# Third attention of a two-block transformer: scores from high and low parts of queries and keys, queries turned one block row ahead

## The reference, cut to what matters

```python
q = (rms_norm_2(c_q, mla_q_norm[j]) @ mla_w_uq[j]).reshape(b, s, N_TOK_HEADS, QK_DIM)
q = jnp.concatenate([q[..., :QK_NOPE], apply_rope(q[..., QK_NOPE:], positions)], axis=-1)
kv = (rms_norm_2(c_kv, mla_kv_norm[j]) @ mla_w_ukv[j]).reshape(
    b, s, N_TOK_HEADS, QK_NOPE + V_DIM)
k_nope, v = kv[..., :QK_NOPE], kv[..., QK_NOPE:]
k_rope = apply_rope(k_r[:, :, None, :], positions)
k = jnp.concatenate(
    [k_nope, jnp.broadcast_to(k_rope, (b, s, N_TOK_HEADS, QK_ROPE))], axis=-1)
tok = causal_attention(q, k, v).reshape(b, s, TOK_WIDTH)
```

```python
sc = jnp.einsum('bqhd,bkhd->bhqk', q_blk, k, preferred_element_type=jnp.float32) * scale
sc = jnp.where(mask[None, None], sc, -jnp.inf)
p = jax.nn.softmax(sc, axis=-1).astype(v.dtype)
return jnp.einsum('bhqk,bkhd->bqhd', p, v)
```

## Time and profile before

| what | value |
|---|---|
| median of 3 runs | 3132.32 us (3131.62 to 3132.63) |
| the profiled execution | 3131.1 us, its span 3129.0 us |
| PE busy | 3066.4 us, 98% of the span |
| DVE busy | 1791.4 us, 57% |
| ACT busy | 1329.6 us, 42% |
| the third attention, first score to last | about 2418.8 to 2705 us of the span |

### The profile page before, as it was taken

How to read it: one execution, slowest core, us unless ns; L and a number is a source line. 1 busy time by engine, 2 the same in 40 slices (tenths; PEclk the granted TensorE clock), 3 DMA queues, 4 the chain that set the end, 5 groups by cost and what they waited for, 6 DMA issues and landing times.

```text
span 3129.0 us, 50323 instructions
## 1 busy us (share of the span) xinstructions
PE 3066.4 (98%) x18600; PEld 2608.8 (83%) x18600; DVE 1791.4 (57%) x3573; ACT 1329.6 (42%) x2637; POOL 664.3 (21%) x886
## 2 busy tenths in 40 slices
PE   7999999999999999999999999998999999999999
PEld 7988888999999888888788888888977777787777
DVE  6657674353344322345888887876353666753675
ACT  5446565454445221232333333454433555522552
POOL 3423334453542000001111111001101011032240
PEclk9999999999999999999999999999999999999999
DMA  5110011011111321122233225643100000221012
GB/s 204 37 48 18 21 35 51 28 62 44 56 59 46 103 78 51 45 95 97 72 109 109 102 101 204 196 151 140 46 28 22 16 28 15 108 72 67 28 61 101
DMA packets 77412, 231.27 MB, mean 74 GB/s; under 512 B 17712, under 2 KB 21936, under 8 KB 65648
## 3 DMA queue, kind: packets, MB, share of 16 engines
q1 hardware_dynamic: 77168, 228.05, 20.8%
HBM read 183.92 MB, written 43.84 MB: 73 GB/s over the span
## 4 chain that ended last, share of the span: by engine, by line
PE 90%; DVE 6%; ACT 2%; issue 1%; DMA 1%; SPq 0%; POOL 0%; DVEq 0%; ACTq 0%; POOLq 0%
PE ps L2546 71%; PE ps L2589 7%; PE ps L2597 3%; PE ps L2553 2%; PE ps L2604 2%; PE ps L2620 2%; PE ps L2612 1%; PE ps L2623 1%; PE ps L2640 1%; DVE wlo L2815 0%; DVE hlo L2892 0%; ACT hhi L2660 0%; ACT whi L2650 0%; DVE qk L2923 0%; DMA fa2r<-scratch_fs 0%
## 5 line engine op out<-in xcount | busy, mean ns | idle before, releaser
L2546 PE MATMUL ps<-whi,hhi 128*128 128x256 f32 (+2 forms) x1920 | 580.5, 302 | 3.0 <-DVE hlo L2892 1.7
L2546 PE MATMUL ps<-whi,hlo 128*128 128x256 f32 (+2 forms) x1920 | 563.7, 294 | 0.0
L2546 PE MATMUL ps<-wlo,hhi 128*128 128x256 f32 (+2 forms) x1920 | 563.4, 293 | 0.0
L2546 PEld LDWEIGHTS ps<-whi,hhi 128*128 128x128 f32 x1920 | 368.2, 192 | 12.8 <-issue 5.1
L2546 PEld LDWEIGHTS ps<-wlo,hhi 128*128 128x128 f32 x1920 | 368.8, 192 | 7.4 <-issue 0.2
L2546 PEld LDWEIGHTS ps<-whi,hlo 128*128 128x128 f32 x1920 | 368.2, 192 | 7.7
L2546 PE MATMUL ps<-hhi,whi 128*128 128x512 f32 x864 | 342.3, 396 | 0.0
L2546 PE MATMUL ps<-hhi,wlo 128*128 128x512 f32 x864 | 337.0, 390 | 0.0
L2546 PE MATMUL ps<-hlo,whi 128*128 128x512 f32 x864 | 336.3, 389 | 0.0
L3154 POOL TENSOR_SCALAR stats<-stats 128x2 f32<-128x2 f32 (+2 forms) x230 | 59.3, 258 | 1194.1 <-ACT xsf L2654 509.1
L3143 POOL CAST whi<-raw 128x512 fp32r<-128x512 f32 (+4 forms) x180 | 113.7, 631 | 865.8 <-PE ps L2546 856.1
(11 more groups left out here) (616 smaller groups left out, 6996.6 us busy)
## 6 DMA issues: line engine op xcount, KB each, us to landing
raw<-in_W SPq DMA_DIRECT2D x61, 1024.0 KB, 4.8
scratch_fs<-fo SPq DMA_DIRECT2D x77, 256.0 KB, 2.0
raw<-in_W SPq DMA_DIRECT2D x24, 768.0 KB, 4.3
wd<-in_WD SPq DMA_DIRECT2D x44, 256.0 KB, 3.5
wf0b<-in_WF SPq DMA_DIRECT2D x10, 1024.0 KB, 5.3
wf1b<-in_WF SPq DMA_DIRECT2D x10, 1024.0 KB, 5.2
scratch_x<-x SPq DMA_DIRECT2D x16, 512.0 KB, 3.3
orw<-scratch_outs SPq DMA_DIRECT2D x6, 1024.0 KB, 5.8
```

Of the source, the lines that this page charges most:

```text
L2546: x = e.matmul(r.out, a, b, start=(r.start and m == 0), stop=(r.stop and m == n - 1), skip_group_check=r.joined)
```

## The change

1. Keys are kept as high and low part: `mkT[z, s, 0]` and `mkT[z, s, 1]`. ACT copies the high part out of PSUM, then DVE subtracts it from PSUM into the low part ("mk_out", and "kr_turn" for the rotated rows that all heads share). Two of the low parts lie in the unused ends of the second weight buffer, so the weights that follow the last projection into that buffer wait for the end of pair 4's scores.
2. Queries are no longer turned in the projection. `mq` is double buffered, and at the start of the scores of each double step `q_turn` turns the two blocks (both heads) of the next double step: PE 2 turns, ACT the high part (96 x 256), DVE the low part (96 x 256).
3. Scores are three passes: high x high, high x low, low x high. For five blocks the pieces are 2+3 instead of 4+1.
4. The turned probabilities are copied by DVE one time in three (`dve_turns=3`), not one in two.
5. The portions of the projections are spread anew over the steps: for odd p every second step, for even p in ten steps in a row.

```diff
@@ Att.probs @@
-                    r.by_dve = self.dve_turns and self.turn % 2 == 1
+                    r.by_dve = self.dve_turns and self.turn % self.dve_turns == 1
@@ q_turn, new @@
+        def q_turn(n):
+            p, qt = n // 8, 7 - n % 8
+            q = Rec()
+            q.place, q.rotated, q.free = DB.take(), q_rotated[p], flat(h_free, kr_places[1].full, q_used.get(n - 2))
+            q.src = [mq[p % 2][:, qt, s * 96:s * 96 + 96] for s in range(2)]
+            q.hi, q.lo = [x[0:96, :] for x in mqT[n % 2]]
+            q.hi_done = signal("mq_hi")
+            emit("mq_turn", q)
+            q_read[n] = q.place.read
@@ proj @@
-                evac(b, [(mkT[z_][s][0:64, cut], b.ps[64 * s:64 * s + 64, :]) for s in range(2)], set_q(p))
+                k = Rec()
+                k.place, k.free, k.hi_done = b, set_q(p), signal("mk_hi")
+                k.hi, k.lo = [[mkT[z_, s, x][0:64, cut] for s in range(2)] for x in range(2)]
+                emit("mk_out", k)
                 yield
-            for s in range(2):
-                for t0 in (0, 4):
-                    q = Rec()
-                    q.place, q.rotated, q.free = DB.take(), r.done, set_q(p)
-                    q.src = [mq[:, t0 + j, s * 96:s * 96 + 96] for j in range(4)]
-                    q.dst = mqT[z_][s][0:96, t0 * 128:t0 * 128 + 512]
-                    emit("mq_turn", q)
-                    yield
@@ units of the third attention @@
-                    for k0 in range(0, qt + 1, 4):
+                    first = 2 if qt == 4 else 4
+                    for k0, n in ((0, min(first, qt + 1)), (first, qt + 1 - first)):
...
+                    if s == 0 and at_q < 47:
+                        u.begin = lambda: q_next(at_q)
@@ fills_m @@
-                for n in range(1 if p % 2 == 0 else 3):
-                    yield
-                yield from proj(p)
-                for n in range(1 if p % 2 == 0 else 3):
+                yield
+                yield
+                for n, _ in enumerate(proj(p)):
+                    yield
+                    if p % 2 and n < 6:
+                        yield
+                for n in range(4 if p % 2 == 0 else 2):
                     yield
@@ steps loop @@
+            if i == 80:
+                spl_free[1] = [p_last[0], pairs[4][-1].s_full]
+                w_split()
@@ tensor, "scores" @@
-                        for p in r.parts:
-                            x = e.matmul(p.place.ps[:, o:o + n], *p.blocks[b], start=True, stop=True)
+                        passes = ((0, 0), (0, 1), (1, 0)) if isinstance(r.parts[0].blocks[b][0], tuple) else (None,)
+                        for j in passes:
+                            for p in r.parts:
+                                q, k = p.blocks[b] if j is None else (p.blocks[b][0][j[0]], p.blocks[b][1][j[1]])
+                                x = e.matmul(p.place.ps[:, o:o + n], q, k, start=j == passes[0], stop=j == passes[-1])
@@ vector, new kinds @@
+                elif kind == "mq_turn":
+                    w.wait_ge(*w.last)
+                    w.wait_ge(*r.hi_done)
+                    e.tensor_tensor(r.lo, r.place.ps[0:96, 0:256], r.hi.bitcast(F), ALU.subtract).then_inc(w.sig(r.place.read), 1)
+                elif kind == "mk_out":
+                    w.wait_ge(*r.hi_done)
+                    for s, (hi, lo) in enumerate(zip(r.hi, r.lo)):
+                        w.wait_ge(*w.last)
+                        a = e.tensor_tensor(lo, r.place.ps[64 * s:64 * s + 64, :], hi.bitcast(F), ALU.subtract)
+                        a.then_inc(w.sig(r.place.read) if s else w.inner(), 1)
```

More of the change, by code:

```diff
@@ L645, in build, with __init__ @@
         class Att:
-            def __init__(self, E, PT, os_, sb, ob, dve_turns=True, together=False, paired=False, by_feature=False, between=False):
+            def __init__(self, E, PT, os_, sb, ob, dve_turns=2, together=False, paired=False, by_feature=False, between=False):
                 self.by_feature, self.between = by_feature, between
@@ L683, in scored @@
                         r.blocks = list(zip(q, rhs)) if isinstance(q, list) else [(q, rhs)]
-                        r.n = sum(k.shape[-1] for _, k in r.blocks)
+                        r.n = sum(width(k) for _, k in r.blocks)
                         r.out, r.mx = u.E[:, at_[x]:at_[x] + r.n], mxs[x][:, p:p + 1]
@@ L2198, in proj @@
                 if hf:
-                    r.done = signal("q_rotated")
+                    r.done = q_rotated[p] = signal("q_rotated")
                     emit("q_rotated", r)
@@ L2224, in proj @@
                 yield
-            ch.done(m)
+            if p == 5:
+                p_last.append(m)
+            else:
+                ch.done(m)
         proj0, kr_places = proj(0), []
@@ L2236, in first_proj @@
             kr_places.append(load("tabM", tabM[:, :], d["tabM"], place.full))
-            kr_places.append([load(f"kr{s}", mkT[1][s][64:96, :], mkT[0][s][64:96, :], place.read, h_free) for s in range(2)])
+            kr_places.append([load(f"kr{s}{x}", mkT[1, s, x][64:96, :].bitcast(F), mkT[0, s, x][64:96, :].bitcast(F), kr_places[0].read, place.read, h_free)
+                              for s in range(2) for x in range(2)])
             yield from proj0
@@ L2242, in build @@
         drain(fill)
-        kr_tok, t_tabM = [kr_places[1].read, kr_places[3]], kr_places[2]
+        kr_tok, t_tabM = [[x.read for x in kr_places[:2]], kr_places[3]], kr_places[2]
         n_done[:] = [mem_us[-1].v_full, mem_us[-1].fin, mem_us[-1].s_full]
-        attM = Att([x[:, :] for x in mE], [x[:, :] for x in mPT], [x[:, :] for x in mO], SB2, OB2, paired=True)
+        attM = Att([x[:, :] for x in mE], [x[:, :] for x in mPT], [x[:, :] for x in mO], SB2, OB2, paired=True, dve_turns=3)
         for s_ in (attM.E, attM.PT, attM.O):
@@ L2586, in _ @@
                     for b in range(len(r.parts[0].blocks)):
[L2587 to L2591 removed]
+                        n = width(r.parts[0].blocks[b][1])
+                        passes = ((0, 0), (0, 1), (1, 0)) if isinstance(r.parts[0].blocks[b][0], tuple) else (None,)
[3 more added lines that the diff above has]
+                                x = e.matmul(p.place.ps[:, o:o + n], q, k, start=j == passes[0], stop=j == passes[-1])
+                                if b == len(p.blocks) - 1 and j == passes[-1]:
+                                    x.then_inc(p.place.full[0], 1)
                         o += n
@@ L2770, in _ @@
                     w.wait_each(r.free)
-                    for x, dst in enumerate(r.dsts):
+                    for x, dst in enumerate(r.dsts[0]):
                         w.wait_ge(*w.last)
                         a = e.activation(dst, r.place.ps[64:96, :], ACT.Copy)
-                        a.then_inc(w.sig(r.place.read) if x == 1 else w.inner(), 1)
+                        a.then_inc(w.sig(r.hi_done) if x == 1 else w.inner(), 1)
                 elif kind == "mq_turn":
@@ L2778, in _ @@
                     w.wait_each(r.free)
-                    e.activation(r.dst, r.place.ps[0:96, :], ACT.Copy).then_inc(w.sig(r.place.read), 1)
+                    e.activation(r.hi, r.place.ps[0:96, 0:256], ACT.Copy).then_inc(w.sig(r.hi_done), 1)
+                elif kind == "mk_out":
+                    w.wait_ge(*r.place.full)
+                    w.wait_each(r.free)
+                    for s, dst in enumerate(r.hi):
+                        w.wait_ge(*w.last)
+                        a = e.activation(dst, r.place.ps[64 * s:64 * s + 64, :], ACT.Copy)
+                        a.then_inc(w.sig(r.hi_done) if s else w.inner(), 1)
                 elif kind == "ln_stats":
```

69 lines of the change are left out of this document (44 added, 25 removed).

## The result

The changed kernel takes 3172.34 us, median of 4 runs (3172.11 to 3175.02), against 3131.97 us for the kernel before beside it (4 runs, 3126.87 to 3132.63). The ratio is 1.0133, with a 95% interval from 1.012 to 1.0146: 40.4 us slower, where 18 were forecast, and beyond the range's end at 3162. The profiled execution has a span of 3170.3 us.

What follows compares the result with a forecast made beforehand. PE bounds the kernel now (98% busy); after, a DVE-ACT loop and key stalls add 2.9 + 2.1 + 2.4 + 2 x 3.1 + 4 + 1 = 18.6 us, PE's gain spent inside: median 3150 us, range 3124 to 3162.

Steps and rivals of the forecast that it cites:

- closed loop: Each double step: exponential, ACT's high part, DVE's low part, next score reading in series; 7.2 us at `qt` = 6, last pair +4.
- a bank wait for the first values' projection adds 1 to 2: 18: Pairs 1 and 3, keys in two steps: DVE's chain 16.6 us plus 1 to 2 of bank wait; +3.1 us each pair.
- the four double steps take 22 us: Pairs 0, 2 and 4, from `qt` = 2 through the next 7: stalls at the keys make 15.3 us of PE work 22.
- at `qt` = 5, given as 8.0: Pairs 0, 2 and 4, double step away from the keys: the larger of loop and PE's work, 8.0 us.
- The start, +1, bounds -1 to +4: Before the first score: wait for turn, high and low part, 1.4 us; fewer turns save PE 1.7; put at +1.
- PE's gain, 16 us: Scores: three fp32r passes instead of two float32 instructions save PE 1.3 us a head, 16 us in all.
- only some 15: Reading of the profile before: DVE has only some 15 us left in a pair, and 9 in the last.
- Rival 1: PE stays the bound, banks and `mE` buffers absorb the loop, the passes pay: 3116 to 3126 us; chance 0.10.
- Rival 2: Loop and gain cancel, the loop binding only in the last pair and at the keys: 3126 to 3138 us; chance 0.12.
- rival 3: Passes of 128 and 384 columns over 96 partitions cost more, or the start stalls 4 us: 3160 to 3175; chance 0.06.
- Rival 4: Passes do not run at fp32r's rate: +47 us, the loop partly beneath it, 3180 us; chance 0.02.

Runs made afterwards that it cites:

- the run with both moves: Changed kernel with keys' high and low parts made by POOL, rotated columns too, and DVE's query subtraction moved behind its unit's score pieces: 3136.9 us, ratio 1.0015.
- the run with queries late: Changed kernel with DVE's subtraction for the next queries' low part moved behind the reductions of its unit's score pieces: 3153.3 us, ratio 1.0072.
- keys spaced: Changed kernel with an empty step behind each half of the projected keys while pairs 1 and 3 are scored: 3164.4 us, ratio 1.0103.

## Why the prediction was wrong, by its own steps

**Right: the direction and the mechanism of the loop.** The closed loop of exponential, high part, low part and next reading is there, and of the length forecast. From the second double step of the last pair, changed kernel:

```profile
2711.37 1.15 ACT L2736 ACTIVATE mE<-mE,stats 128x1024 f32<-128x1024 f32 x1 [0.76 <-DVE stats L2988]
...
2712.64 0.38 ACT L2818 ACTIVATE mqh<-ps 96x256 fp32r<-96x256 f32 x1
2713.12 0.42 DVE L3117 TENSOR_TENSOR mql<-ps,mqh 96x256 fp32r<-96x256 f32 x1 [1.85 <-ACT mqh L2818]
2713.58 0.69 DVE L2978 TENSOR_SCALAR_CACHE_REDUCE mE<-ps 128x512 f32<-128x512 f32 x1
...
2714.33 0.73 PE L2628 MATMUL ps<-mkT,mqh 96*128 96x512 f32 x2 [1.33 <-DVE mE L2978]
...
2720.52 0.42 DVE L3117 TENSOR_TENSOR mql<-ps,mqh 96x256 fp32r<-96x256 f32 x1 [2.00 <-ACT mqh L2818]
```

From one low part to the next are 7.40 us, forecast 7.2; the last pair took 41.1 us, forecast 40. This is also where the earlier trace rows came true in their worse form: there DVE idled 0.69 us for the exponential, here 1.85 and 2.00.

**Wrong: the bank wait in pairs 1 and 3, the start, and a clock that the sum did not have.** By window (us):

| pair | 0 | 1 | 2 | 3 | 4 | 5 | first score |
|---|---|---|---|---|---|---|---|
| forecast | 49.5 | 56 | 51 | 56 | 51 | 40 | +1 |
| measured | 51.9 | 60.8 | 53.5 | 59.8 | 53.4 | 41.1 | +5.7 |

These are 17.0 us in the pairs and 4.7 ahead of them, 21.7 of the 22.3 that are missing.

- *Pairs 1 and 3, "a bank wait for the first values' projection adds 1 to 2: 18"*: the two double steps took 23.0 and 22.3 us. The wait was named and sized at 1 to 2 us; it was 4.4 in both pairs. The step treated DVE's chain (16.6 us) as the bound and priced the bank wait on top of it; the rows show one chain from the exponential's start over two copies to two subtractions, with PE idle for all of it. These two pairs are half of the miss by window, 8.6 of 17.0 us. In pairs 0, 2 and 4 the same wait was forecast at 2.0 us and measured at 2.0, 2.0 and 2.3.
- *The clock.* No term of the sum had it: each price was taken from rows at a clock of 1.00, and a wait was counted as its own length. After a wait the work behind it ran at half clock: 2.65 us of pair 1's 5.9, some 12 us over the attention at most (half of PE's 23.3 busy us at half clock). The Trainium skill, "TensorE: Matmul & The Clock Gate", section "Terms", puts the penalty at the throttled time times the share of clock pulses that do not pass: by that the 24 us more at half than in the run with both moves are an estimated 12. The rows agree where PE is busy in them (11.7 us of busy time more). They do not where it stands still: with ACT's four copies the clock is at half for 10 us more than after, and PE's busy time is the same.
- *Pairs 0, 2 and 4, "the four double steps take 22 us"*: 23.8, 23.1 and 23.3. And at `qt` = 5, given as 8.0, 9.0: the run with queries late has 8.0 there, so this is the loop, which the forecast took to be covered by two portions of projection.
- *The start, +1, bounds -1 to +4*: from the first turn of the rotated keys to the first score are 25.8 us, 20.4 before. Three passes alone have 20.4 there, no low parts of queries and projected keys 23.3. The forecast priced the turn and low part ahead of the first score, and let the keys' subtractions fall where DVE waits anyway. They fell, with the rotation's products, ahead of a copy of turned probabilities of the attention before, for which PE waited:

```profile
2405.58 1.41 DVE L3122 TENSOR_TENSOR mkT<-ps,mkT 64x512 fp32r<-64x512 f32 x2
2407.03 0.42 DVE L3014 COPY nPT<-ps 128x256 f32<-128x256 f32 x1
2407.51 0.69 PE L2636 MATMUL ps<-ident,nE 128*128 128x128 f32 x2 [3.65 <-DVE nPT L3014]
```

  That wait was 0.94 us before and 2.13 without the subtractions, and here the clock is at half for 6.8 us with PE busy for 4.7. So 2.7 us of longer wait and some 2.3 of lower clock are most of the 5.4.
- *PE's gain, 16 us*: 10.0 when alone. A piece was priced at three times the distance between passes (0.69, 0.53, 0.36 and 0.33 us for 512 to 128 columns). That distance is right, but behind turns the second pass starts later than that, by 0.03 us at 128 columns and 0.08 at the others, so that from the first pass to the instruction behind the third there are 0.78, 0.61, 0.44 and 0.37 us:

```profile
2709.77 0.71 PE L2628 MATMUL ps<-mkT,mqh 96*128 96x512 f32 x2
2710.32 0.40 PE L2628 MATMUL ps<-mkT,mql 96*128 96x512 f32 x1
2710.55 0.60 PE L2636 MATMUL ps<-ident,mE 128*128 128x128 f32 x4
```

  A part of it comes back in the turns: with three passes alone, four turns behind a piece take 0.36 us where they took 0.44. The forecast spent the gain within each pair, so this moves the sum little.
- *A reading.* DVE had 16 to 22 us left in the pairs with a projection, not "only some 15".
- *Rivals.* Rival 1 (banks absorb the loop) falls. Rival 2 needed the loop to bind only in the last pair and at the keys; that nearly held in pairs 1 and 3 (double steps of 9.3 us at `qt` = 6 with and without low parts), not at `qt` = 5 of the others. The time lies in rival 3's 3160 to 3175, and its start of over 4 us came true; but its causes give only a small part of the miss. Rival 4 falls: the passes follow each other in 0.23 us, not 0.43.

What stays open: how many of the half-clock stretches would go by shortening one wait alone. The stretches moved from run to run of the variants (27 us behind the first score after, 24 with queries late, 10 with keys spaced), and no run changed the clock by itself, so what it costs is an estimate from rows. Open too is how the keys' 22.6 us are shared between the held bank and DVE's load.

## What to carry to other kernels

When a bank's release gets a second reader, cost the whole chain from the event that ACT waits for to the last reader, not the reader's own duration: TensorE waited 4.4 us for that chain where 1 to 2 were priced, and giving ACT two more copies in place of DVE's reading of the bank freed it hardly sooner and cost 8 us more. Place a subtraction that waits for another engine behind the work that is already ready in its queue (19 us here), unless it holds a bank that TensorE will wait for (7 us lost). And where a forecast finds waits of some microseconds on TensorE, in a kernel that had none, price the work behind them at the lower clock too.

## What the runs showed of the hardware

- TensorE's granted clock fell to 0.50 in this kernel though its share of busy time was 97%. Twice it fell in a wait of 4.4 us (at 2514.6 and 2627.2); four times behind the first score it fell up to 1.1 us after a wait of 1.65 to 2.33 us had ended, with PE at work (at 2466.8, 2473.6, 2589.7 and 2695.5). The same wait of 2.0 us that stood ahead of 2466.8 stood in pair 2, to 2580.9, and no fall came after it. Before, the longest wait from 2396 us to the attention's end was 0.94 us, and there was no fall. At half clock a 256-column pass took 0.21 us in place of 0.12, and 24 matmuls with 64 weight columns 2.83 us, in place of 1.53 in the run without keys' low parts.
- Over 96 partitions an fp32r pass of 512 columns followed another in 0.23 us. A piece of three took 0.78 us behind turns, up to the instruction after it, and two float32 instructions 0.86.
- POOL made high and low part of 64 x 512 keys in 0.60 and 1.27 us from SBUF, beside DVE, and in the run with both moves that cost TensorE 3.2 us of waiting in the attention.
